# Down matrix by columns, in quarters of two halves, and the scatter inside the own job, in a fused transformer and mixture-of-experts block

## The reference

```python
def grouped_moe(x, w_router, router_bias, w_gate, w_up, w_down):
    scores = jax.nn.sigmoid((x @ w_router).astype(jnp.float32))
    ...
    combine = jnp.einsum('btk,btke->bte', gates, jax.nn.one_hot(idx, N_EXPERTS, dtype=jnp.float32)).astype(x.dtype)
    y = jnp.zeros_like(x)
    for e in range(N_EXPERTS):
        h = jax.nn.silu(x @ w_gate[e]) * (x @ w_up[e])
        y = y + combine[..., e:e + 1] * (h @ w_down[e])
    return y
```

## Time and profile before

| | us |
|---|---|
| median of 3 runs | 1449.94 |
| lowest and highest | 1449.91, 1450.63 |
| the profiled execution, own time | 1452.63 |
| its span | 1450.8 |
| TensorE busy | 1297.9 (89%) |
| VectorE busy | 427.2 (29%) |
| ScalarE busy | 206.9 (14%) |
| mean granted TensorE clock | 0.971 |
| DMA | 559.57 MB, 386 GB/s over the span |

### The profile page before, as it was taken

One profiled execution on the slowest core, in us unless ns is written; L12 is line 12 of the kernel. 1 busy time (PEld: TensorE's weight loads), 2 busy tenths in 40 slices (PEclk: granted clock), 3 DMA queues, 4 the chain that ended last, 5 costly groups with the idle time before them and its releaser, 6 DMA issues.

```text
span 1450.8 us, 20436 instructions
## 1 busy us (share of the span) xinstructions
PE 1297.9 (89%) x8678; PEld 619.2 (43%) x8679; DVE 427.2 (29%) x804; ACT 206.9 (14%) x482; POOL 74.9 (5%) x138
## 2 busy tenths in 40 slices
PE   3999999999999996999999999998887877888757
PEld 1656544555454464433632543442432442343223
DVE  2122596777566430202111201121111111111102
ACT  3100101244101142100200110110110110011001
POOL 0012100121132000000000000000000000000000
PEclk9999999999999998999999999999999999999988
DMA  9899868766898899999999999999999999999995
GB/s 392 367 419 389 325 258 329 299 231 240 320 375 344 347 409 394 428 426 385 428 427 419 413 425 428 403 427 427 430 429 428 429 428 428 428 429 428 428 426 243
DMA packets 57019, 559.57 MB, mean 386 GB/s; under 512 B 6640, under 2 KB 6768, under 8 KB 19952
## 3 DMA queue, kind: packets, MB, share of 16 engines
q1 hardware_dynamic: 42048, 502.25, 83.1%
q0 software_dynamic: 14320, 52.01, 9.6%
q10 hardware_dynamic: 576, 4.19, 0.7%
HBM read 556.34 MB, written 2.10 MB: 385 GB/s over the span
## 4 chain that ended last, share of the span: by engine, by line
PE 59%; DMA 33%; DVE 3%; issue 2%; ACT 1%; DVEq 0%; POOL 0%; SPq 0%; ACTq 0%; POOLq 0%
DMA ring<-w_gate_dram 11%; DMA ring<-w_up_dram 11%; PE ps L890 9%; PE ps L599 9%; PE ps L895 9%; PE ps L857 5%; PE ps L914 5%; DMA big<-w_up_dram 4%; DMA ring<-w_half_dram 3%; PE ps L920 3%; PE ps L593 3%; PE ps L711 2%; PE ps L604 2%; DMA ring<-w_in_dram 2%; DMA big<-w_gate_dram 2%
## 5 line engine op out<-in xcount | busy, mean ns | idle before, releaser
L1619 DVE TENSOR_TENSOR big<-ps,big 128x1024 f32<-128x1024 f32 x60 | 70.7, 1219 | 313.3 <-PE ps L843 168.3
L895 PE MATMUL ps<-ring,big 128*64 128x512 f32 x560 | 132.9, 608 | 21.7 <-DMA ring<-w_up_dram 10.6
L599 PE MATMUL ps<-ring,big 128*128 128x512 f32 x320 | 146.9, 601 | 2.5 <-DMA ring<-w_in_dram 2.5
L1254 DVE SCALAR_TENSOR_TENSOR once<-ring,silu_c,once 128x1024 f32<-128x1024 f32 x96 | 123.2, 1283 | 69.8 <-DMA ring<-w_half_dram 64.5
L857 PEld LDWEIGHTS ps<-probs,big 128*128 128x128 f32 x1024 | 119.5, 192 | 44.2 <-issue 37.5
L857 PE MATMUL ps<-probs,big 128*128 128x96 f32 x1024 | 130.0, 280 | 1.9 <-DVE probs L1623 1.9
L890 PE MATMUL ps<-ring,early 128*32 128x256 f32 x1408 | 91.4, 407 | 37.0 <-DMA ring<-w_up_dram 18.3
L711 PE MATMUL ps<-ring,big 128*128 128x512 f32 x240 | 105.0, 593 | 0.0
L599 PEld LDWEIGHTS ps<-ring,big 128*128 128x128 f32 x320 | 59.2, 192 | 72.2 <-issue 66.9
L895 PEld LDWEIGHTS ps<-ring,big 128*64 128x64 f32 x560 | 36.2, 137 | 104.2 <-issue 66.9
L890 PEld LDWEIGHTS ps<-ring,early 128*32 128x32 f32 x1408 | 44.5, 115 | 84.3 <-issue 27.5
(11 more groups left out here) (315 smaller groups left out, 1128.9 us busy)
## 6 DMA issues: line engine op xcount, KB each, us to landing
ring<-w_down_dram SPq DMA_DIRECT2D x48, 2048.0 KB, 22.2
ring<-w_up_dram SPq DMA_DIRECT2D x46, 2048.0 KB, 22.2
ring<-w_gate_dram SPq DMA_DIRECT2D x33, 2048.0 KB, 19.8
ring<-w_half_dram POOLq DMA_DIRECT2D x96, 512.0 KB, 6.8
big<-w_up_dram SPq DMA_DIRECT2D x18, 2048.0 KB, 19.6
ring<-w_mix_dram SPq DMA_DIRECT2D x32, 1024.0 KB, 11.3
late<-w_down_dram SPq DMA_DIRECT2D x16, 2048.0 KB, 22.4
big<-w_gate_dram SPq DMA_DIRECT2D x15, 2048.0 KB, 22.1
```

The costliest lines, as they stand in the source:

```text
L599: mm = pe.matmul(ps[:, b + t, :], nT[:, k, t * P:(t + 1) * P], w, start=(k == 0), stop=(k == KT - 1))
L895: mm = pe.matmul(out_b[1][REST * f:REST * (f + 1), :], rows[1][:, k, :], w[:, kk, f * N:(f + 1) * N], start=(k == 0), stop=(k == KT - 1))
L1254: stt(total, half_slots[:, m % HALF_SLOTS, :], silu_c[:, m % KT, 0:1], total, ALU.mult, ALU.add) \
L1619: tt(y, Yb[:, 2 * h:2 * h + 2, :].rearrange("p a n -> p (a n)"), y, ALU.add).then_inc(summed, 1)
```

## The change

The weights w_down lie in memory by columns: a load of 2 MB holds 512 of the 2048 columns for all 1024 rows, instead of 256 rows for all columns. So a load completes a quarter q of the result. For a quarter, the two halves of 256 columns stand side by side: partitions 0 to 63 hold columns 0 to 255, partitions 64 to 127 the others. In the 32-row part each half has two partial sums, the even and the odd row tiles, 32 rows each; the scatter adds them, as its spread matrix has 64 rows in which each slot stands twice. The gate of the modulation is laid out alike for both parts (`gate_out`).

The scatter goes by quarters, inside the own job: scatter(q - 1) stands behind the first half of quarter q's down product, scatter(3) at the end of the job. A call takes both halves of the tokens, and for each part two products of 256 columns and 64 rows, from partitions 0 to 63 and 64 to 127, into two banks (`Yb`, now 6 and 7). The gather has its own two banks (`Xb`, 4 and 5) and waits for ScalarE (`rows_saved`). VectorE multiplies each quarter by the gate and adds it, four times in a job, and only for the parts that the job has. The spread matrices too are made and transposed for those parts only. Nothing is left to do behind the last job; the output goes out in eight pieces as the last job's quarters are added.

```diff
-            for q, (t, a, b) in enumerate(OUT_PIECES):
-                sp.wait_ge(out_ready, q + 1)
-                sp.dma_start(out[t * P:(t + 1) * P, a:b], total[:, t, a:b]).then_inc(out_sent, 16)
...
+            for q in range(4):
+                for t in range(TT):
+                    sp.wait_ge(summed, jobs * 8 + (2 * q + t + 1))
+                    sp.dma_start(out[t * P:(t + 1) * P, q * N:(q + 1) * N], total[:, t, q * N:(q + 1) * N]) \
+                        .then_inc(out_sent, 16)
...
-                        for q in range(4):
-                            mm = pe.matmul(C[q % 2][REST * (q // 2):REST * (q // 2 + 1), :],
-                                           k_("spread")[:, q * P:q * P + REST], modrow[:, 1, :],
...
+                    for q in (2 * i, 2 * i + 1):
+                        for h in range(2):
+                            mm = pe.matmul(S[i][64 * h:64 * (h + 1), (q % 2) * 256:(q % 2 + 1) * 256],
+                                           k_("spread")[:, q * P:q * P + 64], modrow[:, 1, h * 256:(h + 1) * 256],
...
+            def scatter(j, q, parts, first):
+
+                pe.wait_ge(outs_saved, j * 4 + (q + 1))
+                if q == 0:
+                    pe.wait_ge(spread_saved, j + 1)
+                if q or not first:
+                    pe.wait_ge(summed, j * 8 + (2 * q + 8))
+                for t in range(TT):
+                    for i in parts:
+                        for h in range(2):
+                            rows = slice(64 * h, 64 * (h + 1))
+                            mm = pe.matmul(Yb[:, h, t * 256:(t + 1) * 256], spread_T[i][rows, t, :], outs[i][rows, q, :],
+                                           start=(i == parts[0]), stop=(i == parts[-1]))
+                mm.then_inc(scattered, 1)
+
+            def gather(j, i, one_hot, first=False):
...
-                pe.wait_ge(summed, adds)
+                if i > 1 or not first:
+                    pe.wait_ge(rows_saved, j * 4 + (i + 3))
...
-                        scatter(j, 0, parts=ahead)
...
-                if not first:
-                    scatter(j, 1, parts=ahead)
                 pe.wait_ge(hidden_ready, j + 1)
...
-                for i in range(2):
+                for i in parts:
                     for t in range(TT):
                         mm = pe.transpose(spreads[:, i, t * P:(t + 1) * P], oh_out[i][:, t, :], ident)
...
+                for q in range(4):
+                    if q == 1 and 1 in parts:
                         pe.wait_ge(spread_saved, j + 1)
...
+                    for c in range(2):
+                        w = arrived(16 + 2 * q + c).rearrange("p (k n) -> p k n", k=4)
+                        for i in range(4) if 0 in parts else ():
+                            k = 4 * c + i
+                            at = (k % 2) * P + BASE * (k // 2)
+                            for h in range(2):
+                                to = 64 * h + BASE * (k % 2)
+                                mm = pe.matmul(Db[0][q % 2][to:to + BASE, q // 2, :], hT[0][:, at:at + BASE],
+                                               w[:, i, h * 256:(h + 1) * 256], start=(k < 2), stop=(k >= 6))
+                        for i in range(4) if 1 in parts else ():
+                            k = 4 * c + i
+                            at = (k % 4) * P + REST * (k // 4)
+                            for h in range(2):
+                                mm = pe.matmul(Db[1][q % 2][64 * h:64 * (h + 1), q // 2, :], hT[1][:, at:at + REST],
+                                               w[:, i, h * 256:(h + 1) * 256], start=(k == 0), stop=(k == 7))
+                        mm.then_inc(slot_free, 1)
+                        if c == 0 and q:
+                            scatter(j, q - 1, parts, first)
+                    if place != "second":
+                        for i in ((0, 1), (2,), (3,), ())[q]:
+                            gather(j + (2 if place == "lead" else 1), i, oh_rows, first)
+                scatter(j, 3, parts, first)
...
+                for q in range(4):
+                    cols = slice(q * N, (q + 1) * N)
+                    dve.wait_ge(slot_free, j * JCH + used_job(17 + 2 * q))
+                    for i in parts:
+                        last = tt(outs[i][:, q, :], Db[i][q % 2][:, q // 2, :], gate_out[:, q, :], ALU.mult)
+                    last.then_inc(outs_saved, 1)
+                    dve.wait_ge(scattered, j * 4 + (q + 1))
+                    for t in range(TT):
+                        y = total[:, t, cols].rearrange("p (h n) -> p h n", h=2)
+                        tt(y, Yb[:, :, t * 256:(t + 1) * 256], y, ALU.add).then_inc(summed, 1)
...
-        "w_down": a["w_down"].reshape(NE, 4, 2, P, D).transpose(0, 1, 3, 2, 4).reshape(NE, 4, P, 2 * D),
+        "w_down": a["w_down"].reshape(NE, 8, P, 4, N).transpose(0, 3, 2, 1, 4).reshape(NE, 4, P, 2 * D),
```

More of the change, by code:

```diff
@@ L257, in build @@
         spread_T = [part(spare, 1536 + 256 * i, 256).rearrange("p (t n) -> p t n", t=TT) for i in range(2)]
-        outs = [part(spare2, 0, N), part(spare2, N, 2 * N).rearrange("p (h n) -> p h n", h=2)]
-        hT = [part(spare2, 3 * N, 256), part(bufA, 0, 512)]
+        outs = [part(spare2, 2 * N * i, 2 * N).rearrange("p (q n) -> p q n", q=4) for i in range(2)]
+        hT = [part(bufB, 512, 256), part(bufA, 0, 512)]
         silu_g = [part(bufA, 512, 256), part(work, 0, 512)]
@@ L964, in _ @@
                     any_job(j, False)
-            few = pe.value_load(n_i[0:1, bass.ds(jobs + (JOBS - 1), 1)], min_val=0, max_val=1)
-            pe.wait_ge(xg_ready, jobs)
-            with pe.If(few):
-                scatter(jobs, 0, parts=(0,))
-                scatter(jobs, 1, ps[:, 0:4, :], parts=(0,))
-            with pe.Else():
-                scatter(jobs, 0)
-                scatter(jobs, 1, ps[:, 0:4, :])
         @block.scalar
@@ L1144, in _ @@
             act.activation(rt[:, 1], rt[:, 0], ACT.Sigmoid).then_inc(score_saved, 1)
-            for i, bank in ((0, S[0]), (1, ps[:, 2:4, :])):
+            for i in range(2):
                 act.wait_ge(bcast_done, 5 + i)
-                copy(gate_out[i], bank).then_inc(bcast_saved, 1)
+                copy(early[:, 0, i * N:(i + 1) * N], S[i]).then_inc(bcast_saved, 1)
             for k in range(KT):
@@ L1154, in save_rows_of @@
             def save_rows_of(j, to):
-                for k in range(KT):
-                    if k % 4 == 0:
-                        act.wait_ge(next_gathered, j * 4 + (k // 4 - 3))
-                    at = k % 4 * BLK
-                    last = act.activation(to[:, k, :], Yb[:, k // 4, at:at + BLK], ACT.Identity,
-                                          bias=modcol[:, 3, k, 0:1], scale=scale_ffn[:, k:k + 1])
-                last.then_inc(xg_ready, 1)
+                for i in range(4):
+                    act.wait_ge(next_gathered, j * 4 + (i - 3))
+                    for k in range(4 * i, 4 * i + 4):
+                        at = k % 4 * BLK
+                        last = act.activation(to[:, k, :], Xb[:, i % 2, at:at + BLK], ACT.Identity,
+                                              bias=modcol[:, 3, k, 0:1], scale=scale_ffn[:, k:k + 1])
+                    last.then_inc(rows_saved, 1)
             def job_evac(j, parts, first=False, place=None):
@@ L1629, in hidden_product @@
                     one_hot_rows(j + 1, oh_second)
-                spread_matrix(j, 0, "slots_w" if 1 in parts else "slots_n")
-                spread_matrix(j, 1, "slots_m" if 1 in parts else "slots_0")
-                if not first:
-                    add_rows(j, 0)
+                if 0 in parts:
+                    spread_matrix(j, 0, "slots_w" if 1 in parts else "slots_n")
+                if 1 in parts:
+                    spread_matrix(j, 1, "slots_m")
                 dve.wait_ge(silu_saved, j + 1)
```

110 lines of the change are left out of this document (21 added, 89 removed).

## The result

The changed kernel took 1482.12 us, median of 4 runs (1480.84 to 1486.76), beside 1450.29 for the kernel before on the same chip: ratio 1.0223, 95% interval 1.0200 to 1.0246. Forecast were 1470, slower, within 1458 to 1487. The direction and the range held; the size was 12 us short. The profiled execution took 1486.76 (span 1484.8), the slowest of the four.

A forecast was written before the change was run, and what follows sets the result against it. TensorE was taken to bound the kernel from 516.96 to 923.25 us and in the tail, the weights' stream from 1025.5. +25 on TensorE and -5.3 in the tail gave +20: 1470 against the median 1449.94, range 1458 to 1487.

The forecast's parts named there:

- What paces: Whole kernel: TensorE sets the pace from 516.96 to 923.25 us, the stream of weights from 1025.5, TensorE again in the tail.
- Term 1: Scatter on TensorE until 923.25: pieces of 1.02 and 1.9 us, 39.2 in all against 24.4 before, +14.8 us.
- Term 2: Down product, now 256 columns wide: +0.25 us per 32-row job, +0.3 per 96-row job, +1.9 over the stretch.
- Term 3: TensorE's uncovered waits before the transposes: 0.6 us in a 32-row job, 1.3 in a 96-row job, +5.4 us.
- Term 4: Wait before each job's last scatter: 1.0 us in seven jobs, +7, less 3 for a wait that goes: +4 us.
- terms 1 to 5: TensorE until 923.25: scatter, down, both waits, and fewer spread transposes in 32-row jobs (-1 us): +25 us.
- step 6: TensorE's 11.40 us stop "for issue" behind job 0: stays as long as it is, bounds -6 and +6 us.
- rival C: Loop of 96-row pairs grows: late instruction fetch at two jumps back, 11.4 us each, +23: 1493; chance 0.08.
- Step 8: Tail, from the last up matrix to the end: ends at 1445.5, gain 5.3 us, bounds 3 and 7.

The follow-up runs named there:

- work_many: Kernel before with 15 more unused 128x256 products in the down stage of each of the three 96-row jobs: 1472.6 us, ratio 1.0164.
- work_mid: Kernel before with the same 15 unused products in the down stage of each of the four 64-row jobs instead: 1451.73 us, ratio 1.0007.
- after_shift100: Kernel after with 25 one-column products (100 instructions) in job 0's never-taken branch, moving the loop: 1464.94 us, ratio 1.0108 to the kernel before.
- pad120: Kernel before with its 96-row-pair loop lengthened to 2,586 instructions by 120 unused one-column products, at the old place: 1478.86 us, ratio 1.0207.
- few_last: Kernel before with best's three small edits and the 32-row branch put last on TensorE, right ahead of the loop: 1448.47 us, ratio 0.9990.
- best: Kernel before with three small edits: no gathers after the last job, a later gate-product wait, no unread spread matrix: 1446.51 us, ratio 0.9976.

## Why the prediction was right, and where it fell short

- **What paces** (TensorE until 923, then the weights): shown by work_many (+22.8 for 22.4 of work) and work_mid (+1.9, its interval from -1.6 to +3.6).
- **Term 1, scatter**: 16 pieces of some 1.07 and 12 of 1.92 are 40.2, against 24.4 before: +15.8 where +14.8 was forecast. That the products of 256 columns run side by side, which no row of before showed, was right.
- **Term 2, down**: 128 narrow records take 1.87 + 6 x 1.00 = 7.9 (7.85 forecast), a chunk of a 96-row job 2.88 (2.87).
- **Term 3, waits before the transposes**: 0.55 and 1.1, forecast 0.6 and 1.3. **Term 4, wait ahead of the last scatter**: 0.72 to 0.80 in 32-row and 0.93 in 96-row jobs, seven in 5.9 where 7 was forecast; so +2.9, not +4.
- **The sum of terms 1 to 5** was +25. From the start of job 0 to the end of the third pair, without its exit stop, after_shift100 takes 425.34 - 6.55 = 418.8, before 406.29 - 11.40 = 394.9: +23.9. Its pairs take 125.9 and 126.0, the pair of before plus 6.7 is 126.9. The bounds of this sum were added up wrongly: the terms' own bounds with the tail's give +8 and +40, 1458 and 1490, and with step 6's 6 us 1452 and 1496, not 1455 and 1489.
- **Step 6 and rival C are what fell short.** Step 6 held for job 0's exit (11.76, then 11.39), and that was luck, since eight dead instructions make it 6.62. The sum took the jumps back as free, because they were free before. They cost 4.76 and 4.54, and with the half clock behind them 14 us in these traces. That is the wait that rival C named, at 60% of its price (23 forecast); C was given 8 in 100. Its reason was incomplete: it spoke of the loop's length, and pad120 has the length without the stops at the jumps back. At a given length, the place of the loop decides (7,795 and 7,803 with stops, 7,895 and 7,955 without); whether a shorter loop has such places too is not known, as the loops of 2,106 and 2,111 stood at three places only. That the time fell into the range is luck in part: the range had been cut so as to leave out most of C, and C came true at a price that just fits in. The Trainium skill, "Runtime: NRT & Kernel Launch", Instruction fetch mechanics, says that a taken branch to a page that is not held forces a fetch before execution can go on. The runs agree that far jumps can stop TensorE, but not that every one does: both loops are longer than the 2,048 instructions it gives for TensorE, and only some jumps back stopped. Whether the hint at the loop's start is what spares the others, no run here shows.
- **Step 8, tail**: 7.5 where 5.3 was forecast. The last addition ends 3.0 us before the span does instead of 4.1, and the last scatter starts 21.3 us behind the last up product, not 22.0 (1438.5 - 1416.54). TensorE's last rows, and VectorE's last additions:

```profile
1477.44 1.07 PE L904 MATMUL ps<-ring,once 128*32 128x256 f32 x16
1479.30 1.14 PE L835 MATMUL ps<-once,early 64*128 64x256 f32 x8 [0.80 <-DVE once L1630]
```
```profile
1480.48 1.29 DVE L1635 TENSOR_TENSOR big<-ps,big 128x512 f32<-128x512 f32 x2 [1.31 <-PE ps L835]
```

Together: -7.5 for the tail, +24 for the terms and +14 for the jumps is +30.5, and the medians differ by 31.8. With both kernels shifted by 100 instructions, without stops at the jumps and with nearly the same exit (6.55 and 5.10), the medians 1464.94 and 1444.67 differ by 20.3, and the two intervals leave it between 14 and 26: the forecast's +20 fits as the price of the change itself, and some 12 us more are the price of where it put the loop.

## What to carry to other kernels

Where an engine paces, narrower products cost little in columns, and cutting their use into pieces costs a change of shape and an uncovered wait each; sum those, they came out within 2 us here. A kernel with branches and loops of thousands of instructions can have stops that depend on where the code lies: before an edit is judged by a few per cent, both versions want a second run with the code moved by dead instructions, and the waits "for issue" at every jump read apart. A stage behind which an engine waits for transfers gives little back when it is made shorter: leaving out the gathers of the tail was priced at 5.5 us and gave 1.4.

## What the runs showed of the hardware that was not expected

- The stop at the exit of job 0, by place of the loop: 11.58, 11.40, 11.36, 11.13 and 10.24 at 7,032; 5.94 at 7,131; 5.10 at 7,132; 5.76 at 7,139; 11.76 and 11.39 at 7,795; 6.62 at 7,803; 6.55 at 7,895; 7.16 at 7,955. The distance of the jump changes with the place in these kernels, so the two aren't told apart; with no distance (few_last) the exit has no stop. Eight instructions are enough to go from one size to the other. A packet of the instruction queue is 16 KB here (66 packets, 1.08 MB), and the two sizes may be one late packet or two; that is a guess.
- The stop at a jump back: 4.5 to 5.3 at 7,795 and 7,803 with 2,591 instructions in the loop; none at 7,895 and 7,955 with the same loop; 0.16 at 7,032 with 2,586, which had 7.49 at the loop's exit instead; 0.92 at 7,032 with 2,097 (best). Which places are bad is not explained by these runs.
- Behind each stop of 4.5 us or more TensorE's granted clock is at the lower level for a moment, which costs 1.6 to 2.8 us (5.10: 1.6; 11.40: 2.1; 4.76: 2.55; 7.49: 2.8) and doesn't grow with the stop's length. It can fall behind a shorter one too: in after_shift100 at 654.75, behind waits of 1.12 and 0.95 us, 16 records take 2.70 instead of 1.95.
- A record of 512 columns on the full array costs 0.45 us here (3.63 for 8); the same work as pairs of 64-row products side by side took about half (1.92 for the 16 records of 256 columns).
